# One layer of a convolution / RWKV-7 / mixture-of-experts step: the first modulation rows in two halves, and the column sums of the convolution's norm in four strips

## The chip, the cores and the metric

One core of one Trainium2 chip runs the whole program. Everything is float32. The metric is the device time of one execution in microseconds (us); the kernel before takes 1237.24 us (median of 3 runs, 1237.11 to 1237.88).

## The reference, cut to what matters

Two streams of 128 tokens (prompt and latent, here `g` = 0 and 1) go through one layer. The layer's first product needs the modulated input `h`:

```python
mod = (silu(c) @ ada_w + ada_b).reshape(6, D)      # D = 1024; one row of conditioning per stream
sh1, sc1, gt1, sh2, sc2, gt2 = mod
h = rms_norm(x, pre_mix_g) * (1.0 + sc1) + sh1
proj = h @ w_in                                    # 2560 columns: conv value and gate, r, k, v
...
a = sigmoid(a0[d] + (h @ a1[d]) @ a2[d])           # low-rank maps w1, a1, g1: 384 columns in all
g = sigmoid(h @ g1) @ g2
...
mu = mean(u, axis=-1); var = mean((u - mu)**2, axis=-1)   # layer norm of the convolution, 512 channels
...
x = x + gt2 * rms_norm(routed_ffn(h2), post_ffn_g)  # 32 experts, each token takes 4
```

`routed_ffn` reads 12 MB of weights per expert (8 MB gate and up, 4 MB down), 384 MB in all.

## The kernel before, in words

There are five instruction streams with semaphores between them and no planner: the order on each engine is the order of the code. SyncE (`SP`) starts nearly all transfers, in program order. TensorE (`PE`) runs all products; a float32 product appears in the trace as two matmul records, a transpose as one.

**First stage (0 to 49 us).** `SP` loads `x0`, then the first 2048 columns of `ada_w` in 8 chunks of 1 MB (`ada0`, line 363; columns 0 to 1023 give the shift, 1024 to 2047 the scale), then `lora1` (1.5 MB, line 365), the small tables, and the five blocks of `w_in` (line 377). PE transposes the normalised input (line 674) and the bias and gain rows (line 680), then takes each `ada_w` chunk with four products that write 32 partitions each (line 687: `siluT` has 32 columns, and product `j` writes rows `32j` to `32j+31` of bank 0, so the four sit in four column strips of the array and run at the same time). The result is copied (DVE line 1488), turned by four small products (line 699) and combined on DVE (lines 1491, 1494) into `modT`, which holds per channel the scale and the shift. Then ACT (line 1117) and DVE (line 1500) make the 8 chunks of `hT` = scale times input plus shift, and PE multiplies them with `lora1` (line 707: two of three 128-column blocks; line 726: the third). ACT puts the three results into `mids` with tanh, copy and sigmoid (line 1140), and PE goes on with the second low-rank factors (line 733), whose 16 results ACT takes one by one (lines 1142, 1144). Then comes `h @ w_in` (line 746). `keep_clock` (line 694) is a product whose result nobody reads.

**Middle (49 to 319 us).** Projections, then four rounds `q` of the RWKV recurrence. A round inverts a triangular matrix in levels `lv` = 1 to 6 (lines 849, 858, 859 on PE; ACT line 1192 and DVE line 1659 take the results). Round `q = 3` also holds the convolution's layer norm: `conv_sum` (line 784) sums 4 blocks of 286 columns over all 128 partitions with four products on a matrix of ones, once for the mean (ahead of level 3) and once for the variance (in level 6). ACT takes the square root (line 1199), DVE the reciprocal (line 1702), scales (lines 1705, 1708), and ACT applies the sigmoid (line 1208).

**Experts (319 us to the end).** 32 experts in pairs; PE line 626 is gate and up, line 664 down. `SP` starts a transfer into a buffer once PE has used it (lines 345, 348, 351).

Of the kernel before, what the change touches and what calls it, by code (L numbers as in the profile page):

```python
# [24 lines left out]
P = 128  # L25
G = 2
# [74 lines left out]
def build(nc, x_in, cond_in, ada_w, mod_in, w_in, w_out, chan_in, lora1_in, w2_in, a2_in, g2_in,  # L101
          s0_in, router_w, router_b, w_gu, b_gu, w_down, b_down, const_in, level_in, part_in,
          y_prompt, y_sample, st_f, st_b):
    with ExitStack() as ctx:
# [54 lines left out]
        first_T = view(r_ra[:, 1024:1088], "p (n m j r) -> p n m j r", n=2, m=4, j=4)  # L159
        madd, mmul = (view(r_hT[:, 1024 * n:1024 * (n + 1)], "p (b n) -> p b n", b=2) for n in range(2))  # L160
# [60 lines left out]
        cvT = view(r_E[:, 0:1024], "p (q t) -> p q t", q=Q)  # L221

# [366 lines left out]
        def pe_pair(pe, base, i, last_pair=False, turn=0, late=(), first=False):  # L589
# [4 lines left out]
            for q in range(2):  # L594
                arrived, arrived_dn = n * 128 + (64 * q + 80), n * 16 + (64 - 16 * q + (0 if first else 16))
# [15 lines left out]
                for k in order:  # L611
# [3 lines left out]
                    if in_spare:  # L615
                        pe.wait_ge(in_gu[3 + k], 80)
                    if first and q == 1 and k == order[-1]:
                        pe.wait_ge(in_gu[7], 80)
                    if q in late and k in (2, 6):
                        pe.wait_ge(in_gu[2 if k == 2 else 3], turn * 96 + (32 * (2 * last_pair + q) + 16))  # L620
                    if last_pair and k == 7 and q == 1:
                        pe.wait_ge(in_gu[4], turn * 32 + 48)
# [46 lines left out]
        def _(pe):  # L669
            pe.wait_ge(s["in_const"], 16)  # L670
# [6 lines left out]
            pe.wait_ge(s["in_mod"], 64)  # L677
# [4 lines left out]
            last.then_inc(s["first_tr"], 1)  # L682
            pe.wait_ge(s["silu"], 1)
# [7 lines left out]
            def keep_clock(count):  # L691

                for _ in range(count):
                    pe.matmul(ps[7], ident, xn[:, 0, 0:512], start=True, stop=True)

            keep_clock(1)
            pe.wait_ge(s["mod0"], 1)
            for m in range(4):
# [1237 lines left out]
```

## Time and profile before

| | |
|---|---|
| median of 3 runs | 1237.24 us |
| the profiled execution, its time | 1238.3 us |
| its span (first to last instruction) | 1236.5 us |
| PE busy | 94% of the span |
| DMA share, mean rate | 9 tenths in most of the slices, 369 GB/s |
| chain that ended last | PE 52%, DMA 43%, DVE 3%, the rest 2% |
| largest wait in that chain | DMA into `ring` from `w_gu`, 38% |

The profiled execution is 1.8 us longer than its span. The chain that ended last is followed back from the last instruction to what released it at each step; the 40 slices of the page are 30.9 us each.

### The profile page before, as it was taken

What the parts mean: (1) busy time and instruction counts of PE and PEld (TensorE: products, weight loads), DVE (VectorE), ACT (ScalarE), POOL (GpSimd) and SP (SyncE); (2) the same over time, 40 slices, a digit from 0 to 9 for tenths busy, and PEclk for the clock granted to TensorE, in tenths of its full rate; (3) what the DMA queues carried; (4) which work ended last, traced back from release to release, by engine and by line L of the source; (5) the groups of instructions that cost most, each with busy time, mean ns of one, the idle gap of its engine ahead of it and who ended that gap; (6) DMA issues with size and microseconds to landing.
All of it is one profiled execution on the core that took longest, in us unless ns stands there. A gap on an engine that the chain in (4) does not pass through costs nothing.

```text
span 1236.5 us, 15201 instructions
## 1 busy us (share of the span) xinstructions
PE 1157.3 (94%) x6032; PEld 549.0 (44%) x6032; DVE 412.6 (33%) x939; ACT 201.9 (16%) x447; POOL 89.1 (7%) x120
## 2 busy tenths in 40 slices
PE   5999999999999999999999898999999998989997
PEld 2886898784443433233333333333433333333332
DVE  0598878765412121212212121212131221212123
ACT  2311334242211101010101111010101011111102
POOL 1002654330000000000000000000000000000000
PEclk9999999999999999999999999999999999999999
DMA  9900724667999999999999999999999999999996
GB/s 370 387 21 29 312 108 171 274 215 267 349 420 425 429 430 429 432 435 430 427 436 426 434 431 425 438 408 423 429 434 429 430 434 428 431 430 426 425 426 262
DMA packets 40086, 456.43 MB, mean 369 GB/s; under 512 B 5056, under 2 KB 5584, under 8 KB 16496
## 3 DMA queue, kind: packets, MB, share of 16 engines
q1 hardware_dynamic: 39256, 455.01, 87.8%
q0 software_dynamic: 480, 0.80, 0.2%
q8 instruction: 25, 0.41, 0.1%
q10 hardware_dynamic: 312, 0.11, 0.0%
q14 instruction: 13, 0.11, 0.0%
HBM read 454.56 MB, written 1.34 MB: 369 GB/s over the span
## 4 chain that ended last, share of the span: by engine, by line
PE 52%; DMA 43%; DVE 3%; issue 1%; ACT 1%; SPq 0%; DVEq 0%; ACTq 0%
DMA ring<-in_w_gu 38%; PE bank L626 24%; PE bank L664 5%; PE bank L746 4%; DMA front<-in_w_down 3%; DMA ring<-in_ada_w 2%; PE bank L849 2%; PE bank L859 2%; PE bank L960 2%; PE bank L581 1%; PE bank L858 1%; PE bank L571 1%; PE bank L756 1%; PE bank L741 1%; PE bank L798 1%
## 5 line engine op out<-in xcount | busy, mean ns | idle before, releaser
L626 PE MATMUL bank<-ring,front 128*64 128x512 f32 x2032 | 461.3, 609 | 35.4 <-DMA ring<-in_w_gu 35.4
L626 PEld LDWEIGHTS bank<-ring,front 128*64 128x64 f32 x2032 | 144.0, 140 | 350.4 <-issue 284.1
L1443 DVE TENSOR_SCALAR front<-bank 128x512 f32<-128x512 f32 x32 | 22.1, 691 | 481.0 <-PE bank L626 481.0
L664 PE MATMUL bank<-front 128*64 128x512 f32 x512 | 113.6, 595 | 9.5 <-ACT front L1091 9.1
L664 PE MATMUL bank<-ring,front 128*64 128x512 f32 x512 | 113.4, 595 | 5.1 <-ACT front L1091 5.1
L1083 ACT ACTIVATE front<-front 128x512 f32<-128x512 f32 x32 | 20.2, 631 | 487.4 <-DVE front L1443 487.4
L1467 DVE COPY front<-bank 64x512 f32<-64x512 f32 x32 | 21.9, 683 | 175.1 <-PE bank L664 175.1
L664 PEld LDWEIGHTS bank<-front 128*64 128x64 f32 x512 | 36.3, 137 | 76.5 <-issue 73.3
L664 PEld LDWEIGHTS bank<-ring,front 128*64 128x64 f32 x512 | 36.3, 137 | 71.9 <-issue 70.4
L581 PE MATMUL bank<-front 128*128 128x512 f32 x136 | 62.9, 605 | 1.1 <-DVE front L1467 1.1
L1561 DVE SCALAR_TENSOR_TENSOR front<-front 128x286 f32<-128x286 f32 x120 | 58.8, 538 | 0.5
L571 PE MATMUL bank<-front 128*128 128x128 f32 x480 | 56.1, 275 | 0.0
L746 PE MATMUL bank<-front,ring 128*128 128x256 f32 x256 | 55.5, 379 | 0.0
L1094 ACT ACTIVATE front<-bank 64x512 f32<-64x512 f32 x32 | 19.0, 593 | 223.6 <-PE bank L664 223.6
L571 PEld LDWEIGHTS bank<-front 128*128 128x128 f32 x480 | 54.8, 192 | 0.0
L746 PEld LDWEIGHTS bank<-front,ring 128*128 128x128 f32 x256 | 48.6, 190 | 6.9 <-ACT front L1144 0.3
L1659 DVE TENSOR_TENSOR ring<-bank,front 128x256 f32<-128x256 f32 x96 | 39.3, 420 | 21.8 <-PE bank L859 14.2
L581 PEld LDWEIGHTS bank<-front 128*128 128x128 f32 x136 | 24.4, 189 | 39.3 <-issue 39.3
L1378 POOL TENSOR_TENSOR ring<-ring,front 128x256 f32<-128x256 f32 x48 | 36.3, 770 | 66.8 <-DVE ring L1651 57.1
L1420 DVE TENSOR_TENSOR front<-front,bank 128x512 f32<-128x512 f32 x64 | 39.4, 677 | 0.0
L849 PE MATMUL bank<-ring 128*128 128x128 f32 x192 | 37.6, 281 | 0.3
L859 PE MATMUL bank<-ring 128*128 128x128 f32 x192 | 36.6, 277 | 0.0
(259 smaller groups left out, 1000.0 us busy)
## 6 DMA issues: line engine op xcount, KB each, us to landing
ring<-in_w_gu SPq DMA_DIRECT2D x46, 4096.0 KB
front<-in_w_down SPq DMA_DIRECT2D x30, 2048.0 KB, 19.5
ring<-in_w_down SPq DMA_DIRECT2D x28, 2048.0 KB, 20.2
ring<-in_w_gu SPq DMA_DIRECT2D x25, 2048.0 KB
ring<-in_ada_w SPq DMA_DIRECT2D x24, 1024.0 KB, 10.3
ring<-in_w_gu SPq DMA_DIRECT2D x20, 1024.0 KB
ring<-in_w_in SPq DMA_DIRECT2D x5, 2048.0 KB, 19.8
ring<-in_w_down SPq DMA_DIRECT2D x6, 1024.0 KB, 9.6
```

The lines of the kernel that those rows point to most:

```text
L571: last = pe.matmul(ps[4 + c // 4][:, (c % 4) * P:(c % 4 + 1) * P], h2[:, g, c * P:(c + 1) * P], sel[:, g].rearrange("p q s -> p (q s)"), s ...
L581: pe.matmul(ps[4 + 2 * g + c], GT[:, g, :], outp[:, c * 512:(c + 1) * 512], start=not on_sums, stop=True, skip_group_check=on_sums).then_i ...
L626: last = pe.matmul(ps[r][64 * hf:64 * hf + 64, :], xT[:, k, S * q:S * q + S], rows, start=False, stop=(k == order[-1]))
L664: last = pe.matmul(ps[2][64 * c:64 * c + 64, :], actT[:, m, 64 * hf:64 * hf + 64], wdn[q][hf][:, m, c * 512:(c + 1) * 512], start=(k == 0) ...
L746: last = pe.matmul(out[:, 0:N], win[kind][:, k, q * P:(q + 1) * P], hT[:, k, :], start=(k == 0), stop=(k == KC - 1))
L849: pe.matmul(ps[c % 2][:, 0:T], LTn[:, lv % 2, g, h, :], YX[:, c, 1, :], start=True, stop=True) .then_inc(s["p_mm"], 1)
L859: pe.matmul(ps[2 + c][:, 0:T], Pn[:, c, :], YX[:, c, 0, :], start=False, stop=(lv == LEVELS - 1), skip_group_check=True).then_inc(s["e_mm" ...
L960: last = pe.matmul(ps[2 * g + c], lhs, wout[:, k, c * 512:(c + 1) * 512], start=(k == 0), stop=(k == KC - 1))
L1378: po.tensor_tensor(LTn[:, lv % 2, g], LT[:, g, :, 0, 3, :], level_mask[lv - 1].unsqueeze(1).broadcast_to([P, 2, T]), ALU.mult).then_inc(s[ ...
L1420: v.tensor_tensor(yacc[:, g, c * 512:(c + 1) * 512], yacc[:, g, c * 512:(c + 1) * 512], ps[4 + 2 * g + c], ALU.add).then_inc(s["y_added"], 1)
L1561: v.scalar_tensor_tensor(acc[:, c, :], u[:, c, tap:tap + A_COLS], wcol, acc[:, c, :], ALU.mult, ALU.add).then_inc(s["conv"], 1)
L1659: v.tensor_tensor(YX[:, c], ps[2 + c][:, 0:2 * T].rearrange("p (a t) -> p a t", a=2), side_mask[lv].unsqueeze(1).broadcast_to([P, 2, T]), ...
```

## The change

Three things, and what hangs on them:

1. **`ada_w` in halves.** `SP` loads the scale half of each of the 8 chunks (0.5 MB each), then `lora1`, then the 8 shift halves, each behind a wait for the scale half of its chunk. ACT's transfer of the bias and gain rows becomes 8 pieces instead of 4. PE makes the scale rows, `hT` is first made without the shift, and `lora1` is multiplied with that. The products of the shift half stand between those of `lora1`. The missing part, shift times `lora1`, is a row of 384 numbers per stream (`brow`): PE makes it in four strips from `shP` and `lora1`, ACT copies it, and three products add it to the three accumulators. DVE adds the shift to `hT` itself afterwards, for `w_in`. `k`, `r` and `v` of `w_in` now wait for both halves.
2. **Column sums in strips.** `conv_sum` becomes `conv_part` (four products of 32 output partitions each) and, after a copy by ACT, `conv_sum(n)` (one product that adds the strips). DVE subtracts the mean one level later.
3. Counts of shared semaphores are raised where the expert part waits on the same ones.

The core of the diff (the raised counts and the renamed views are left out):

```diff
@@ SyncE
-                sp.dma_start(ada0[:, k, :], ada_w[k * P:(k + 1) * P, 0:2048]).then_inc(in_ada0[k], 16)
+                sp.dma_start(ada0[:, k, D:2 * D], ada_w[k * P:(k + 1) * P, D:2 * D]).then_inc(in_ada0[k], 16)
             for hf in range(2):
                 sp.dma_start(lora1[:, 4 * hf:4 * hf + 4, :], lora1_in[:, 4 * hf:4 * hf + 4, :])\
                     .then_inc(s["in_lora_b" if hf else "in_lora"], 16)
+            for k in range(KC):
+                sp.wait_ge(in_ada0[k], 16)
+                sp.dma_start(ada0[:, k, 0:D], ada_w[k * P:(k + 1) * P, 0:D]).then_inc(in_ada0[k], 16)
...
-                    sp.wait_ge(s["ada0_acc"], KC)
+                    sp.wait_ge(s["ada0_acc"], 2 * KC)
@@ TensorE
+            def condition(k, at):
+                for j in range(4):
+                    last = pe.matmul(ps[0][32 * j:32 * j + 32, at:at + 256], siluT[:, k, :],
+                                     ada0[:, k, 4 * at + 256 * j:4 * at + 256 * j + 256],
+                                     start=(k == 0), stop=(k == KC - 1), skip_group_check=True)
+                last.then_inc(s["ada0_acc"], 1)
...
             for k in range(KC):
                 pe.wait_ge(in_ada0[k], 16)
-                for j in range(4):
-                    last = pe.matmul(ps[0][32 * j:32 * j + 32, :], siluT[:, k, :], ada0[:, k, j * 512:(j + 1) * 512],
-                                     start=(k == 0), stop=(k == KC - 1), skip_group_check=True)
-                last.then_inc(s["ada0_acc"], 1)
+                condition(k, 256)
+            keep_clock(ps[7])
             pe.wait_ge(s["mod0"], 1)
+            turn_rows((2, 3))
+            keep_clock(ps[7])
...
                 for n in range(2):
+                    pe.matmul(bank_of(n)[:, 0:N], lora1[:, k, n * P:(n + 1) * P], hT[:, k, :], start=(k == 0), stop=False)
+                shifts(*{3: (0,), 5: (1,), 7: (2, 3)}.get(k, ()))
+            for k in range(KC):
+                pe.matmul(bank_of(2)[:, 0:N], lora1[:, k, 2 * P:3 * P], hT[:, k, :], start=(k == 0), stop=False)
+                shifts(*{1: (4,), 4: (5,), 7: (6, 7)}.get(k, ()))
+            keep_clock(ps[1])
+            pe.wait_ge(s["mod0"], 2)
+            turn_rows((0, 1))
+            keep_clock(ps[1], 256)
+            pe.wait_ge(s["modT"], 2)
+            for k in range(KC):
+                t = k % 4
+                last = pe.matmul(ps[0][32 * t:32 * t + 32, 0:3 * P], shP[:, k, :], lora1[:, k, :],
+                                 start=(k < 4), stop=(k >= 4), skip_group_check=True)
+            last.then_inc(s["mod0_tr"], 1)
+            keep_clock(ps[1], 256)
+            pe.wait_ge(s["in_rw"], 32)
+            pe.wait_ge(s["mod0"], 3)
+            for n in range(3):
+                pe.matmul(bank_of(n)[:, 0:N], brow[:, n * P:(n + 1) * P],
+                          const[:, K_E2:K_E2 + G].unsqueeze(2).broadcast_to([P, G, T]), start=False, stop=True)\
+                    .then_inc(s["l2_mm"], 1)
...
-                    last = pe.matmul(ps[7][:, 0:A_COLS], ones, src[:, q, :], start=(q == 0), stop=(q == Q - 1))
+                    last = pe.matmul(ps[7][32 * q:32 * q + 32, 0:A_COLS], ones[:, 0:32], src[:, q, :], start=True, stop=True)
+            def conv_sum(n):
+                pe.wait_ge(s["c_std"], n)
+                pe.matmul(ps[7][:, 0:A_COLS], one_of_32, cpart, start=True, stop=True).then_inc(s["cs_mm"], 1)
@@ ScalarE
-                             scale=modT[:, m, 2 * (2 + hf):2 * (2 + hf) + 1],
-                             bias=modT[:, m, 2 * hf:2 * hf + 1]).then_inc(s["hT_a"], 1)
+                             scale=modT[:, 2 + m, G * j:G * j + 1]).then_inc(s["hT_a"], 1)
+            a.wait_ge(s["mod0_tr"], 3)
+            a.activation(brow, ps[0][:, 0:3 * P], ACT.Copy).then_inc(s["mod0"], 1)
...
+                        if q == Q - 1 and (lv, c) in ((3, 0), (LEVELS - 1, 2)):
+                            a.wait_ge(s["cs_mm"], 1 if lv == 3 else 3)
+                            a.activation(cpart, ps[7][:, 0:A_COLS], ACT.Copy).then_inc(s["c_std"], 1)
@@ VectorE
+            v.wait_ge(s["ada0_acc"], 2 * KC)
+            v.tensor_copy(mod0[:, 0:256], ps[0][:, 0:256]).then_inc(s["mod0"], 1)
...
+            for c in range(0, KC, 2):
+                two = hT[:, c:c + 2, :].rearrange("p c (g t) -> p c g t", g=G)
+                v.tensor_tensor(two, two, shP[:, c:c + 2, 0:G].unsqueeze(3).broadcast_to([P, 2, G, T]), ALU.add)\
+                    .then_inc(s["hT_v"], 1)
```

How it moves PE's instructions. In the first stage before, PE's queue between the last conditioning chunk and the first products of `lora1` (L707; the last word of a row names what it waits for, `in_wide_k` is the semaphore of chunk `k`):

```order
L687 MATMUL bank<-ring,front 32x512 [waits in_wide_7]
L687 MATMUL bank<-ring,front 32x512 x3
L694 MATMUL bank<-front 128x512
L699 MATMUL bank<-front 128x8 [waits mod0]
L699 MATMUL bank<-front 128x8 x3
L694 MATMUL bank<-front 128x512
L707 MATMUL bank<-front 128x256 [waits hT_v,hT_a,in_lora]
```

In the change, the end of the same stage, from the last two shift chunks (L698) to the second low-rank factors (L767):

```order
L698 MATMUL bank<-ring,front 32x256 [waits in_wide_6]
L698 MATMUL bank<-ring,front 32x256 x3
L698 MATMUL bank<-ring,front 32x256 [waits in_wide_7]
L698 MATMUL bank<-ring,front 32x256 x3
L679 MATMUL bank<-front 128x512
L706 MATMUL bank<-front 128x8 [waits mod0]
L706 MATMUL bank<-front 128x8
L679 MATMUL bank<-front 128x256
L741 MATMUL bank<-front 32x384 [waits modT]
L741 MATMUL bank<-front 32x384 x7
L679 MATMUL bank<-front 128x256
L748 MATMUL bank<-front 128x256 [waits mod0,in_rw]
```

The copy, the turning and the way back from DVE stood once, ahead of the products of `lora1`; now they stand twice, and the second time a further product (L741), ACT's copy of it and a third step on PE (L748) follow before the low-rank stage can go on.

In round 3, level 6, PE's queue around the variance before (L849 is a level's first product, L859 its last; L784 the sum):

```order
L849 MATMUL bank0<-ring 128x128 [waits p_ev,ltn,yx_ev]
L784 MATMUL bank7<-front 128x286 [waits c_sq]
L784 MATMUL bank7<-front 128x286 x3
L859 MATMUL bank2<-ring 128x128 [waits p_ev]
L849 MATMUL bank1<-ring 128x128 [waits p_ev,ltn,yx_ev]
```

and in the change (L820 the strips, L826 the sum of the strips, L890 and L900 the level's products):

```order
L890 MATMUL bank0<-ring 128x128 [waits p_ev,ltn,yx_ev]
L820 MATMUL bank7<-front 32x286 [waits c_sq]
L820 MATMUL bank7<-front 32x286 x3
L900 MATMUL bank2<-ring 128x128 [waits p_ev]
L890 MATMUL bank1<-ring 128x128 [waits p_ev,ltn,yx_ev]
L900 MATMUL bank3<-ring 128x128 [waits p_ev]
L826 MATMUL bank7<-front 128x286 [waits c_std]
```

The four products stay where they were, with 32 output partitions instead of 128, and one product with a wait for ACT's copy (`c_std`) comes in three products later.

## Rows read from the trace of the kernel before

**Rows 1.** The page: slices of 30.9 us, and the chain that ended last.
```profile
PEclk9999999999999999999999999999999999999999
DMA  9900724667999999999999999999999999999996
...
PE 52%; DMA 43%; DVE 3%; issue 1%; ACT 1%; SPq 0%; DVEq 0%; ACTq 0%
```

**Rows 2.** Windows: us; busy (count) of PE, PEld, DVE, ACT, POOL; PEclk, DMA share, GB/s.
```profile
324.00:327.00 3.00, 3.00 (x18) 1.00 (x16) 0.00 (x0) 0.00 (x0) 0.00 (x0) 1.00 0.98 309
330.00:333.00 3.00, 3.00 (x16) 0.77 (x12) 0.69 (x1) 0.01 (x1) 0.00 (x0) 1.00 1.00 423
```

**Rows 3.** Timeline, 0 to 60 us: start us, us, engine, line, op, count [idle before].
```profile
1.68 1.48 ACTq L1102 DMA_DIRECT2D front<-in_mod  x4
...
5.96 1.06 ACT L1108 ACTIVATE front<-front 128x1024 f32<-128x1024 f32 x1 [1.25 <-DMA front<-in_x]
...
8.30 1.28 ACT L1111 ACT_TABLE_LOAD   x1
9.60 0.29 ACT L1111 ACTIVATE front<-front 128x2 f32<-128x2 f32 x1
...
16.86 4.50 PE L687 MATMUL bank<-ring,front 128*32 128x512 f32 x40
...
18.17 0.13 PEld L687 LDWEIGHTS bank<-ring,front 128*32 128x32 f32 x4 [0.30 <-issue]
18.60 0.13 PEld L687 LDWEIGHTS bank<-ring,front 128*32 128x32 f32 x4 [0.30 <-issue]
...
25.26 1.94 PE L687 MATMUL bank<-ring,front 128*32 128x512 f32 x8 [1.42 <-DMA ring<-in_ada_w]
...
27.75 1.94 PE L687 MATMUL bank<-ring,front 128*32 128x512 f32 x8 [0.56 <-DMA ring<-in_ada_w]
...
29.75 0.69 DVE L1488 COPY front<-bank 128x512 f32<-128x512 f32 x1 [12.44 <-PE bank L687]
...
32.58 0.19 DVE L1491 TENSOR_TENSOR front<-bank,front 128x32 f32<-128x32 f32 x1 [2.14 <-PE bank L699]
...
33.65 7.14 PE L707 MATMUL bank<-front 128*128 128x256 f32 x32
...
40.46 0.76 ACT L1140 ACTIVATE front<-bank 128x256 f32<-128x256 f32 x2 [4.47 <-PE bank L707]
40.63 3.62 PE L726 MATMUL bank<-front 128*128 128x256 f32 x16
41.23 1.28 ACT L1140 ACT_TABLE_LOAD   x1
44.28 0.38 ACT L1140 ACTIVATE front<-bank 128x256 f32<-128x256 f32 x1 [1.77 <-PE bank L726]
...
44.81 4.48 PE L733 MATMUL bank<-front 64*128 64x256 f32 x32 [0.57 <-ACT front L1140]
```

**Rows 4.** Windows, columns as in rows 2, of the first stage.
```profile
14.70:24.80 10.10, 7.72 (x67) 3.23 (x65) 0.35 (x3) 0.00 (x0) 0.00 (x0) 1.00 1.02 424
24.90:31.60 6.70, 5.79 (x20) 1.36 (x20) 0.69 (x1) 0.00 (x0) 0.00 (x0) 0.50 1.01 405
31.80:40.00 8.20, 8.05 (x39) 6.51 (x39) 3.02 (x10) 2.90 (x8) 0.48 (x2) 1.00 1.05 386
```

**Rows 5.** One line's durations: ns min/median/max, where strips and whole-array products change places.
```profile
L756 PE MATMUL bank<-ring,front x128: 592/592/617, 149.5 to 230.0; 128*32 128x512 f32 x128
L969 PE MATMUL bank<-front x8: 590/592/697, 304.5 to 308.9; 128*128 128x512 f32 x8
```

**Rows 6.** Timeline, narrow: the change from strips to the whole array, and back.
```profile
16.45 0.47 PE L680 MATMUL bank<-front 8*128 8x8 f32 x3
16.86 1.07 PE L687 MATMUL bank<-ring,front 128*32 128x512 f32 x8
...
306.35 0.64 PE L987 MATMUL bank<-front 128*32 128x128 f32 x16
...
306.93 0.70 PE L969 MATMUL bank<-front 128*128 128x512 f32 x1
```

**Rows 7.** Timeline, 250 to 271 us: the two column sums and what follows.
```profile
251.06 2.09 PE L784 MATMUL bank<-front 128*128 128x286 f32 x8
...
262.17 2.10 PE L784 MATMUL bank<-front 128*128 128x286 f32 x8
...
264.52 1.53 DVE L1662 TENSOR_TENSOR ring<-bank,front 128x256 f32<-128x256 f32 x4 [2.20 <-PE bank L859]
...
264.92 0.49 ACT L1199 ACTIVATE front<-bank,front 128x286 f32<-128x286 f32 x1
...
265.97 1.93 DVE L1702 RECIPROCAL front<-front 128x286 f32<-128x286 f32 x1
```

More of the change, by code:

```diff
@@ L669, in _, with keep_clock @@
         def _(pe):
+            def keep_clock(bank, cols=512):
+                pe.matmul(bank[:, 0:cols], ident, xn[:, 0, 0:cols], start=True, stop=True)
             pe.wait_ge(s["in_const"], 16)
@@ L682, in _, with turn_rows, shifts @@
             last.then_inc(s["first_tr"], 1)
+            def condition(k, at):
[4 more added lines that the diff above has]
+                last.then_inc(s["ada0_acc"], 1)
+            def turn_rows(ms):
+                for m in ms:
+                    last = pe.matmul(ps[0][:, m * 8:(m + 1) * 8], mod0[:, m * P:(m + 1) * P], used_rows, start=True, stop=True)
+                last.then_inc(s["mod0_tr"], 1)
+            def shifts(*chunks):
+                for k in chunks:
+                    pe.wait_ge(in_ada0[k], 32)
+                    condition(k, 0)
             pe.wait_ge(s["silu"], 1)
@@ L685, in _ @@
                 pe.wait_ge(in_ada0[k], 16)
-                for j in range(4):
-                    last = pe.matmul(ps[0][32 * j:32 * j + 32, :], siluT[:, k, :], ada0[:, k, j * 512:(j + 1) * 512],
-                                     start=(k == 0), stop=(k == KC - 1), skip_group_check=True)
-                last.then_inc(s["ada0_acc"], 1)
[L691 to L696, printed above, removed]
+                condition(k, 256)
+            keep_clock(ps[7])
             pe.wait_ge(s["mod0"], 1)
-            for m in range(4):
-                last = pe.matmul(ps[0][:, m * 8:(m + 1) * 8], mod0[:, m * P:(m + 1) * P], used_rows, start=True, stop=True)
-            last.then_inc(s["mod0_tr"], 1)
-            keep_clock(1)
+            turn_rows((2, 3))
+            keep_clock(ps[7])
+            pe.wait_ge(s["modT"], 1)
             for k in range(KC):
@@ L723, in _ @@
                         pe.wait_ge(s["kk"], emptied(n - 7, "v"))
-                if kind == "l1":
-                    for k in range(KC):
-                        last = pe.matmul(out[:, 0:N], lora1[:, k, q * P:(q + 1) * P], hT[:, k, :],
-                                         start=(k == 0), stop=(k == KC - 1))
-                elif kind in "wa":
+                if kind in "wa":
                     pe.wait_ge(s["in_lora2"], 48)
@@ L907, in _ @@
                         level_update(q, lv, 1)
+                        if lv == 3 and q == Q - 1:
+                            conv_sum(1)
                         level_product(q, lv, 3)
@@ L1101, in _ @@
             for j in range(4):
-                a.dma_start(first[G * j:G * j + G], mod_in[:, 32 * j:32 * j + G, 0:512].rearrange("n r c -> r n c"))\
-                    .then_inc(s["in_mod"], 16)
+                for half in range(2):
+                    r, c = 32 * (2 * half + j // 2), 256 * (j % 2)
+                    a.dma_start(first[G * j:G * j + G, :, 256 * half:256 * half + 256],
+                                mod_in[:, r:r + G, c:c + 256].rearrange("n r c -> r n c")).then_inc(s["in_mod"], 16)
             a.wait_ge(s["in_cond"], 16)
@@ L1294, in _ @@
             po.memset(siluT, 0.0).then_inc(s["silu_pad"], 1)
+            po.memset(shP, 0.0).then_inc(s["silu_pad"], 1)
             po.memset(r_u, 0.0)
@@ L1692, in _ @@
                         norm_bonus(q - 1)
-                    if q == Q - 1 and lv in (2, 3):
-                        v.wait_ge(s["cs_mm"], 1)
-                        for c in (2 * lv - 4, 2 * lv - 3):
+                    if q == Q - 1 and lv in (3, 4):
+                        v.wait_ge(s["cs_mm"], 2)
+                        for c in (2 * lv - 6, 2 * lv - 5):
                             v.scalar_tensor_tensor(acc[:, c, :], ps[7][:, 0:A_COLS], -1.0 / CH, acc[:, c, :],
```

74 lines of the change are left out of this document (41 added, 33 removed).

## The prediction, before the run

> **What bounds the kernel now.** I read the page first: DMA is at nine tenths from slice 10 to the end, and the chain that ended last is PE and DMA alone [rows 1]. So the question is where the DMA stream of the experts starts. The windows from 324 us show it at 0.98 and then 1.00 of its share while PE still runs without a pause [rows 2]: from 330 us on the queue is never empty, each of its early transfers is released by PE, and PE before 319 us is what releases the first. A microsecond that PE's chain gains or loses before 319 us moves the end by a microsecond; nothing the change does after that point moves anything. Second I read the timeline of the first stage, where the change works. PE waits there for `ada_w`: chunks come every 2.49 us (25.26 and 27.75), the last at 27.75, and between its end at 29.69 and the first product of `lora1` at 33.65 lie a copy, the turning and DVE's steps [rows 3]. PE ran much of that at the lower clock: the granted clock was 1.00 to 24.8 us, 0.50 from 24.9 to 31.6 us, and 1.00 again after (2.4, 1.2 and 2.4 GHz) [rows 4]. From 33.65 to 44.25 us PE is busy with `lora1`, and the second low-rank factors start at 44.81 us [rows 3]. That start is the mark for the first stage: what follows it is the same in both kernels. Third I read the timeline of round 3, where both column sums stand in PE's queue with nothing beside them, 2.1 us each, and the second is followed by the square root and the reciprocal at 265.97 us [rows 7].
>
> **The change, first stage.** All times are those of the profiled execution.
>
> *Start of the scale half.* Eight chunks of 0.5 MB instead of 1 MB free 4 x 2.49 = 10.0 us of transfer: the last lands at 27.75 - 10.0 = 17.8 us. PE is then the later one. It reaches the first chunk at 16.86 us; a round of four strips over 512 columns takes 0.43 us (18.17 to 18.60) [rows 3], over 256 columns 0.215 us. Eight chunks of two rounds are 3.44 us, to 20.3 us. The tail of a product is 0.16 us (592 ns long, 430 ns apart) [rows 3, 5]. Copy, turning and DVE: `keep_clock` holds PE until 20.3 + 0.2 + 0.86 = 21.4 us, four turning records of 0.11 us and the tail lead to 22.0 us, and from DVE's start to the first product of `lora1` it is 33.65 - 32.58 = 1.07 us as before [rows 3]. `lora1` starts at 23.1 us, 10.5 us earlier than before, and both its halves (3.7 us behind the scale half at 424 GB/s [rows 4]) are there by 21.6 us. The four more pieces of bias and gain rows lie on ACT: four took 1.48 us, and ACT then waited 1.25 us for `x0` [rows 3], so I cost them at nothing; without that cover they would be 1.5 us.
>
> *What gives it back.* (a) The same products of `lora1` take 7.14 and 3.62 us less one overlap, 10.4 us to the last start-to-start step [rows 3]. (b) The shift half's 16 rounds are now on the path and no longer under a transfer: 3.44 us. (c) Its chunks stand in six groups, and each group is a change from whole-array products to strips and back. What a change costs is seen in three places. Into strips: three records 0.11 us apart begin at 16.45 us, so 16.79 us was due and 16.86 us came [rows 6], and the first round takes 617 instead of 592 ns [rows 5]; elsewhere it is some 20 ns more, so 0.12 us. Out of strips: L987's four rounds of 0.11 us end their steps at 306.83 us, the next product starts at 306.93 us [rows 6] and is 697 instead of 592 ns long [rows 5], so 0.20 us. Six times in and five times out until the last shift round are 1.7 us. The stream ends at 23.1 + 10.4 + 3.4 + 1.7 = 38.7 us. The last shift chunk lands at 21.6 + 10.0 = 31.6 us, well before it is due, at about 38 us. (d) The second way round: `keep_clock` and its entry to 39.8 us, turning and DVE to 40.75 us, strips of 384 columns (four rounds of 0.32 us, with entry and tail 1.6 us) to 42.3 us, ACT's copy of 384 columns with its wait 0.55 us (a little over the 0.49 us of 286 columns [rows 7]), the way back to PE 0.15 us as from 44.66 to 44.81 us [rows 3]: the three adding products start at 43.0 us. (e) The first of them is through at 43.6 us and ACT takes two blocks in 0.76 us, to 44.4 us. Then comes a cost that was hidden: the table load of 1.28 us ran at 41.23 us under the third block's 3.62 us of products [rows 3]. What follows a load starts at once (8.30 + 1.28, and 9.60 us [rows 3]). Now the three results come 0.43 us apart and nothing covers it. 44.4 + 1.28 + 0.38 + 0.15 = 46.3 us against 44.81 us: the first stage **loses 1.5 us**.
>
> The adding of the shift to `hT` is four DVE instructions of 512 columns, 0.7 us each as the copy of 512 [rows 3], from 41 us; the first product that needs it comes near 50 us, so it costs nothing, and if that cover were gone 2.8 us. `SP` waits for a scale chunk before each shift chunk, with `lora1` queued behind that chunk; the bytes ahead of `w_in` are the same, so its blocks land as before, and `k`'s longer wait (from 29.7 to 38.9 us) ends while the two blocks ahead of it still run.
>
> Of the change between strips and whole products the trace gives 0.3 us a pair, by which six groups, the `shP` strips and both column sums cost 2.9 us. The Trainium skill, TensorEngine Tiling (Array Packing), section "Key Properties", says that changing the tiling mode, and not just the tile, drains TensorE; it gives no figure. Taken as one tail of 0.16 us for every change, an estimate from the rows, the six groups and the two sums would cost 18 x 0.16 = 2.9 us: rule and row agree here, and a sum made as if strips were free would put the first stage at a gain of 0.5 us instead.
>
> **The change, column sums.** Eight records of 286 columns take 1.93 us (2.10 less the tail) [rows 7], 0.24 us each. Now two rounds of strips are 0.48 us, in and out 0.32 us, and the adding product 0.48 us: 1.28 us, a gain of 0.65 us for the first. The second is followed by DVE: before, PE's first update waited out the whole sum, and the reciprocal began 3.8 us after the sum's start (262.17 to 265.97) [rows 7]. Now that update starts after 0.8 us, DVE takes four results of 0.38 us (1.53 us for four [rows 7]), the third held up by the adding product, and the reciprocal begins after 3.1 us, with the square root (0.49 us [rows 7]) just ahead of it: 0.7 us. ACT's two copies of 0.43 us lie in its pauses. Together a **gain of 1.35 us**. The bounds: nothing, if copies and waits eat it; 2.0 us, if strips cost nothing to enter and leave.
>
> **Sum.** +1.5 - 1.35 = +0.15 us. The profiled execution would take 1238.3 + 0.15 = 1238.45 us; it stood 1.1 us above the median, so the median becomes **1237.4 us**. The smallest difference I count as one is 0.2%, 2.5 us.
>
> **The rivals.**
> - *Strips are nearly free.* If the reloading of the weights is hidden in the change's longer rounds, the first stage gains 0.5 us and the sums 2.0 us: 1234.7 us, faster. For it: four weight loads lie inside each round. Against: every change of form in rows 5 and 6 shows a price. Chance 0.12.
> - *The clock falls (the other side, slower).* PE would have nothing between about 44.5 and 46.3 us while ACT loads its table, and short pauses in the second way round before it; then come the `w_in` products, which are bound by PE. Before, the clock fell after pauses of 1.4 us in every 2.5 us and stayed at 0.50 for 6.8 us [rows 3, 4]. The same stretch, if PE were busy in all of it, would cost half of itself, 3.4 us: 1240.8 us. It makes the kernel slower by over 0.2% from 4.7 us at the lower level on. Against: that fall followed several pauses in a row, this is one. Chance 0.10.
> - *The second way round is longer than I count* (each step between engines 0.2 us more, ten steps, or ACT's copies in level 3 and 6 hold PE): +2 us, 1239.4 us, still within 0.2%. Chance 0.18.
> - *The change doesn't do what it says:* a chunk of half the bytes needs the same 2.49 us. The last shift chunk would land at 31.5 + 8 x 2.49 = 51.4 us and the mark at 59 us: +14 us, 1251 us. Against: `w_in`, which comes in rows of 2 KB, runs at 386 GB/s [rows 4], the halves have 4 KB. Chance 0.02.
>
> **How the numbers follow.** The forecast has 0.58 and 1236.3 to 1238.6 us for itself. From 1235.2 to 1240.2 us lie the forecast, the third rival and part of the first two; 0.2 is left out. Faster by over 0.2% (below 1234.8): most of the first rival, 0.10. Slower by over 0.2% (above 1239.7): the second and fourth rival and a tail of the third, 0.16. Within: 0.74.
>
> **What would show it.** Right: the first product of `lora1` near 23 us, the last shift round near 38.7 us, ACT's table load in the open, the second factors' start (mark) near 46.3 us, the reciprocal 3.1 us after the variance strips, the granted clock 1.00 from 14.7 us to the experts, DMA full from 330 us. Wrong: a mark before 45 us, a reciprocal that is under 2.7 us or over 3.8 us behind the strips, a clock of 0.50 between 40 and 55 us, or a pause of PE before a shift chunk that DMA ends.

## The result, and the profile after

| | before | changed |
|---|---|---|
| median (lowest to highest), runs | 1237.22 us (1235.37 to 1242.09), 20 | 1239.46 us (1237.05 to 1246.03), 20 |
| the profiled execution, its time | 1238.3 us | 1243.65 us |
| its span | 1236.5 us | 1241.9 us |

The ratio is 1.0022 with an interval of 1.0012 to 1.0032: 2.2 us longer between the medians, where +0.15 us was forecast. The median lies inside the outer range of the forecast (1235.2 to 1240.2 us) and outside the 1236.3 to 1238.6 us that the forecast had for itself. It equals the 1239.4 us of the third rival by luck, since the second way round, which that rival makes longer, takes what the forecast gave it (see below). The profiled execution is far from the median of its kernel this time, and the runs of the change lie in two groups: eleven of the twenty from 1237.05 to 1239.51 us, nine from 1241.36 to 1246.03 us, none between. The profile is of the upper group, and so it shows what a median hides.

The page of the changed kernel, the lines that answer to [rows 1]:

```profile
PEclk9999999999999999999999999999999999999999
DMA  9900734567999999999999999999999999999995
...
PE 57%; DMA 38%; DVE 3%; ACT 1%; issue 1%; SPq 0%; DVEq 0%; ACTq 0%
```

The bound is the same: DMA is full from slice 10 on. At that scale nothing else can be seen; the clock line reads 9 throughout. The timeline of the changed kernel, TensorE and ACT in the first stage (start us, us, engine, line, operation, count, idle before it and what ended it), answers to [rows 3]:

```profile
11.93 3.65 PE L685 MATMUL bank<-front 128*128 128x128 f32 x16 [11.93 <-DVE front L1533]
15.50 3.58 PE L691 MATMUL bank<-front 8*128 8x8 f32 x16
19.01 5.73 PE L698 MATMUL bank<-ring,front 128*32 128x256 f32 x64
...
24.67 1.13 PE L679 MATMUL bank<-front 128*128 128x512 f32 x2
...
27.28 3.69 PE L729 MATMUL bank<-front 128*128 128x256 f32 x16 [0.18 <-ACT front L1164]
...
47.20 1.54 PE L748 MATMUL bank<-front 128*128 128x256 f32 x6
...
48.75 1.28 ACT L1189 ACT_TABLE_LOAD   x1
...
50.57 4.49 PE L767 MATMUL bank<-front 64*128 64x256 f32 x32 [1.82 <-ACT front L1189]
```

The mark, the start of the second low-rank factors, is at 50.57 us (L767) instead of 44.81 us: +5.76 us, where +1.5 us was forecast. Read it in pieces. From the first product of `lora1` (L729) to the mark it is 50.57 - 27.28 = 23.29 us; the forecast had 46.3 - 23.1 = 23.2 us. That part holds. The first product itself is 4.2 us late, at 27.28 instead of 23.1 us, and the reason stands in the first three rows. The 16 transposes (L685), the 16 products that turn the bias and gain rows (L691) and the 64 strip records of the scale half (L698) run one after the other with no pause and no wait, and simply take long: 3.65, 3.58 and 5.73 us. The forecast had taken 16.86 us for the start of the strips and 3.44 us for their rounds.

Whether that is the clock can be read in the steps of L698. Two windows of the same timeline, 22.6 to 23.1 us and 23.4 to 23.7 us; a row lists every record that runs in its window, so the two rows share some:

```profile
22.00 1.45 PE L698 MATMUL bank<-ring,front 128*32 128x256 f32 x12
```
```profile
22.85 1.03 PE L698 MATMUL bank<-ring,front 128*32 128x256 f32 x12
```

Both are three rounds of four records. Less the tail of 0.16 us the first three take 1.29 us, 0.43 us each, the other three 0.87 us: one of 0.43 and two of 0.22 us. So TensorE went from 1.2 to 2.4 GHz at 23.3 us. The view of windows gives 1.00 for all of this stretch; up to the first change in an execution that column does not show the level, and the durations do (here 0.43 us for a round at 1.00, and 0.22 us for the same round at 1.00).

The end of the first half, in narrow windows of the timeline of TensorE around the first expert product, before and then changed:

```profile
319.12 0.65 PE L626 MATMUL bank<-ring,front 128*64 128x512 f32 x2
```
```profile
323.53 0.65 PE L633 MATMUL bank<-ring,front 128*64 128x512 f32 x2
```

From the mark to the first expert product it is 274.31 us before and 272.96 us now: -1.35 us, the forecast gain of the column sums to the hundredth. And DMA starts as before, later by the same amount. The changed kernel, windows laid 4.4 us after those of [rows 2]:

```profile
328.40:331.40 3.00, 3.00 (x18) 1.00 (x16) 0.00 (x0) 0.00 (x0) 0.00 (x0) 1.00 1.00 314
334.40:337.40 3.00, 3.00 (x16) 0.77 (x12) 0.69 (x1) 0.01 (x1) 0.00 (x0) 1.00 1.03 434
```

The spans differ by 5.4 us: +5.76 in the first stage, -1.35 in the middle, +1.0 in the expert part (917.4 us before, 918.4 us now). That last part is the same code; over all profiles of this study it takes between 915.6 and 918.5 us with no relation to the kernel, so a single span says little about differences under some 3 us. The starts of single products say more.

The theory to test: **the terms of the sum are right, and what was missed is when the clock rises.** The rivals: the strips cost something else than 0.3 us a pair; ACT's table load is not what delays the mark; the strips in the column sums cost something in the experts' part.

### The profile page after: what moved, and what is told of

Read it like the earlier page. It is cut to its first block, busy times and chain, and to the rows that moved or that the text cites. A ratio compares the mean times of both kernels' runs of the same rounds, so it can differ in the third digit from the quotient of the medians.

```text
span 1241.9 us, 15419 instructions
## 1 busy us (share of the span) xinstructions
PE 1163.7 (94%) x6128; PEld 552.6 (44%) x6128; DVE 415.0 (33%) x945; ACT 202.5 (16%) x450; POOL 89.6 (7%) x121
## 4 chain that ended last, share of the span: by engine, by line
PE 57%; DMA 38%; DVE 3%; ACT 1%; issue 1%; SPq 0%; DVEq 0%; ACTq 0%
DMA ring<-in_w_gu 35%; PE bank L633 25%; PE bank L671 6%; PE bank L782 4%; DMA front<-in_w_down 3%; PE bank L588 2%; PE bank L900 2%; PE bank L890 2%; PE bank L1005 2%; PE bank L899 1%; PE bank L578 1%; PE bank L792 1%; PE bank L775 1%; PE bank L839 1%; PE bank L613 1%
## 5 line engine op out<-in xcount | busy, mean ns | idle before, releaser
L890 PE MATMUL bank<-ring 128*128 128x128 f32 x192 | 37.7, 282 | 0.3
L900 PE MATMUL bank<-ring 128*128 128x128 f32 x192 | 36.6, 277 | 0.0
```

What stands on the lines that cost most here:

```text
L890: pe.matmul(ps[c % 2][:, 0:T], LTn[:, lv % 2, g, h, :], YX[:, c, 1, :], start=True, stop=True) .then_inc(s["p_mm"], 1)
L900: pe.matmul(ps[2 + c][:, 0:T], Pn[:, c, :], YX[:, c, 0, :], start=False, stop=(lv == LEVELS - 1), skip_group_check=True).then_inc(s["e_mm" ...
```

## The experiments

Times of first products are read from each kernel's timeline. "Expert" is the first expert product, "full" the moment from which TensorE's steps are those of 2.4 GHz; in the last column the medians, each with its ratio to the kernel before on the same chip. The kernel before was run again beside each set: its median was 1237.24 us beside the second run of the changed kernel and e1 to e3, 1237.12 us beside e4 to e7, 1236.67 us beside e8 and e9. The ratio is estimated from all runs and differs a little from the quotient of two medians.

| kernel | full from | first `lora1` product | mark | expert | median us, ratio |
|---|---|---|---|---|---|
| before | 14.6; 1.2 GHz 24.9 to 31.7 | 33.65 | 44.81 | 319.12 | 1237.22 |
| changed | 23.3 | 27.28 | 50.57 | 323.53 | 1239.46, 1.0022 [1.0012, 1.0032] |
| changed, again | 24.5; 1.2 GHz 51.8 to 55.2 | 27.78 | 51.07 | 325.06 | 1239.55, 1.0020 [1.0005, 1.0034] |
| e1 | 9.6 | 21.59 | 44.88 | 317.85 | 1237.79, 1.0001 [0.9990, 1.0012] |
| e2 | 23.8 | 31.80 | 42.96 | 315.94 | 1236.75, 1.0000 [0.9984, 1.0016] |
| e3 | 14.7 | 23.09 | 46.38 | 320.75 | 1242.99, 1.0037 [1.0021, 1.0053] |
| e4 | 10.2; 1.2 GHz 27.3 to 37.6 | 35.74 | 47.73 | 322.03 | 1239.13, 1.0005 [0.9991, 1.0020] |
| e5 | 11.2 | 21.60 | 43.22 | 316.16 | 1235.15, 0.9982 [0.9970, 0.9995] |
| e6 | 11.7 | 21.68 | 43.67 | 316.61 | 1235.46, 0.9988 [0.9977, 0.9999] |
| e7 | 11.4 | 21.57 | 41.88 | 314.83 | 1234.49, 0.9972 [0.9960, 0.9983] |
| e8 | 12.8 | 32.83 | 44.00 | 318.34 | 1238.07, 1.0012 [1.0001, 1.0022] |
| e9 | 9.8 | 32.61 | 43.78 | 316.75 | 1237.19, 1.0002 [0.9992, 1.0012] |

**The changed kernel again**, with no edit.

> The changed kernel once more, to see the granted clock of the first stage in a second profile. Theory A (cold start: everything PE does from its first transposes on is now on the path, at whichever clock it is granted, where before a wait for ada_w hid it): the start of the second low-rank factors (the mark) lies between 45.1 us (clock full from the first product) and 50.6 us (full only from 23 us on), and it moves with the moment of the rise; the median is 1237.5 to 1241 us. Rival B (the loss is in the expert part, not ahead of it): the mark is near 50.6 us in every profile whatever the clock, and the time from the first expert to the end differs from before by over 1 us.

The late rise is no accident of one execution: strips at 18.76 us, full from 24.5 us, first `lora1` product at 27.78 us. The mark, at 51.07 us, is 0.5 us outside the expected stretch, because the clock rose 1.2 us later still. Both profiles rose late, so this run alone doesn't separate the theory from rival B; the time from the first expert product to the end (917.8 us, before 917.4 us) speaks against the rival, and e1 and e3 decide. Again two groups: seven of twelve runs up to 1239.8 us, five from 1241.42 us, and again the profiled one (1244.81 us) is of the upper. This execution also shows what the forecast's second rival had in mind. Two views of this kernel: the timeline at the mark, and the windows view of a stretch that begins 0.8 us after it:

```profile
51.07 1.55 PE L767 MATMUL bank<-front 64*128 64x256 f32 x8 [1.82 <-ACT front L1189]
```
```profile
51.90:55.10 3.20, 3.20 (x18) 3.20 (x17) 2.57 (x16) 3.17 (x9) 0.00 (x0) 0.50 1.05 388
```

The granted clock is 0.50 for 3.4 us. From the mark to the first expert product it takes 273.99 us instead of 272.96: the fall cost 1.0 us. None of the other profiles of the changed order has it at this place (changed, e1, e3, e5, e6, e7), although the pause ahead of the mark is the same 1.82 or 1.83 us in four of them.

**e1: TensorE busy before the first rows.** Eleven products that nobody reads, ahead of the transposes, while TensorE has nothing to do.

```diff
             pe.wait_ge(s["in_const"], 16)
+            for _ in range(11):
+                pe.matmul(ps[7][:, 0:P], ident, ident, start=True, stop=True)
             pe.wait_ge(s["xn"], 2)
```

> The changed kernel with 11 products of ident with itself ahead of the transposes, as soon as ident is loaded; their result is read by nobody. Theory A: the clock is full before or during the transposes, 16 transposes take about 1.9 us instead of 3.65, the turned rows 2.0 instead of 3.6 us, the mark comes at 45 to 46.5 us, and the median falls by 2 to 4 us against the changed kernel, to about 1236.3 us, with a smaller spread. Rival B: mark and median stay.

The timeline of this kernel, the rows that answer to those of the changed kernel:

```profile
6.47 4.18 PE L683 MATMUL bank<-front 128*128 128x128 f32 x22 [6.47 <-DMA front<-in_const]
11.61 1.97 PE L687 MATMUL bank<-front 128*128 128x128 f32 x16 [0.96 <-DVE front L1535]
13.51 1.95 PE L693 MATMUL bank<-front 8*128 8x8 f32 x16
15.38 3.66 PE L700 MATMUL bank<-ring,front 128*32 128x256 f32 x64
...
21.59 3.69 PE L731 MATMUL bank<-front 128*128 128x256 f32 x16 [0.18 <-ACT front L1166]
...
44.88 1.44 PE L769 MATMUL bank<-front 64*128 64x256 f32 x10 [1.83 <-ACT front L1191]
```

The three stretches take 1.97, 1.95 and 3.66 us instead of 3.65, 3.58 and 5.73 us: the same instructions at the other level of the clock. From there the distance is that of the changed kernel (21.59 to 44.88 us: 23.29 us in both). The mark falls from 50.57 to 44.88 us, and the runs lie within 1.9 us (1237.02 to 1238.90) instead of 9.0 us: the upper group is gone, and it stays away in e5, e6 and e7, which have the same eleven products (36 more runs, each kernel within 3.9 us). This is what the theory said. The mark is 0.1 us below the expected 45 to 46.5 us. The median, 1237.79 us, is 1.8 us below that of the changed kernel beside it, where 2 to 4 us were expected. Against the kernel before it is no gain (ratio 1.0001), although the first expert product comes 1.27 us earlier than in before's profile. That may lie in the expert part, which varies by up to 2.9 us between profiles, or in executions of before that were not profiled; that is not settled.

**e2: the column sums alone,** on the kernel before.

```diff
-                    last = pe.matmul(ps[7][:, 0:A_COLS], ones, src[:, q, :], start=(q == 0), stop=(q == Q - 1))
+                    last = pe.matmul(ps[7][32 * q:32 * q + 32, 0:A_COLS], ones[:, 0:32], src[:, q, :], start=True, stop=True)
...
+                pe.wait_ge(s["c_std"], n)
+                pe.matmul(ps[7][:, 0:A_COLS], one_of_32, cpart, start=True, stop=True).then_inc(s["cs_mm"], 1)
```

> The kernel before with the column sums in strips alone. Theory A and the prediction's second term: 1.35 us less up to the first expert (317.8 instead of 319.2 us in the trace), ratio 0.9989, the reciprocal 3.1 us behind the start of the variance strips. Rival C (the sums' gain is eaten by ACT's copies or lost before the experts): no difference at the first expert, ratio 1.000.

Mark to expert is 315.94 - 42.96 = 272.98 us, again 1.33 us less than before: the gain stands on its own in the trace. The runs can't show it: the ratio is 1.0000 with an interval of 0.9984 to 1.0016, which holds the expected 0.9989 and the rival's 1.000 alike. The surprise is in the first stage, which is that of the kernel before, to the instruction. The timeline of e2:

```profile
11.69 3.65 PE L676 MATMUL bank<-front 128*128 128x128 f32 x16 [11.69 <-DVE front L1494]
15.26 3.58 PE L682 MATMUL bank<-front 8*128 8x8 f32 x16
18.77 8.71 PE L689 MATMUL bank<-ring,front 128*32 128x512 f32 x56
27.75 1.06 PE L689 MATMUL bank<-ring,front 128*32 128x512 f32 x8 [0.27 <-DMA ring<-in_ada_w]
...
31.80 7.14 PE L709 MATMUL bank<-front 128*128 128x256 f32 x32
...
42.96 0.88 PE L735 MATMUL bank<-front 64*128 64x256 f32 x5 [0.56 <-ACT front L1151]
```

Here the clock rose late too, and it did no harm: TensorE is behind the chunks for 8.7 us, works them off (x56 without a pause) and has caught up at 27.75 us, when the last chunk lands as in [rows 3]. And it never paused ahead of that chunk, and the clock did not fall at 24.9 us (that the two belong together is tested in e8): the last eight strips take 1.06 instead of 1.94 us, and the mark is at 42.96 instead of 44.81 us. So between these profiles a late rise is worth a gain of 1.85 us in the old order, and a loss of 4.2 us in the new one. The profiled execution is near the fastest of its kernel (1233.93 us, lowest 1233.56). The twelve runs reach up to 1241.64 us, and those of before, 34 beside these, from 1235.26 to 1241.12 us. Two profiles 1.85 us apart don't account for such a spread; where it comes from in the old order is open.

**e3: the first stage alone.** The changed kernel with the column sums put back.

```diff
-                    last = pe.matmul(ps[7][32 * q:32 * q + 32, 0:A_COLS], ones[:, 0:32], src[:, q, :], start=True, stop=True)
+                    last = pe.matmul(ps[7][:, 0:A_COLS], ones, src[:, q, :], start=(q == 0), stop=(q == Q - 1))
```

> The changed kernel with the column sums as before (the first stage's change alone). Prediction's terms with theory A: 1.35 us more than the changed kernel at the same clock, so 1239 us when the clock rises early and up to 1243.5 us when it rises late. Rival C: the same as the changed kernel.

By chance this profile caught an early rise (14.7 us, as in the profile of before), without any added product. Its timeline:

```profile
11.68 3.40 PE L685 MATMUL bank<-front 128*128 128x128 f32 x16 [11.68 <-DVE front L1521]
15.01 1.95 PE L691 MATMUL bank<-front 8*128 8x8 f32 x16
16.89 3.66 PE L698 MATMUL bank<-ring,front 128*32 128x256 f32 x64
20.48 1.12 PE L679 MATMUL bank<-front 128*128 128x512 f32 x2
...
23.09 3.69 PE L729 MATMUL bank<-front 128*128 128x256 f32 x16 [0.18 <-ACT front L1155]
...
46.38 1.31 PE L767 MATMUL bank<-front 64*128 64x256 f32 x9 [1.83 <-ACT front L1180]
```

23.09 and 46.38 us, against 23.1 and 46.3 us of the forecast: with the clock that the forecast assumed, its sum comes out. The runs are again in two groups, four of eleven from 1238.16 to 1239.29 us, the profiled one (1238.68 us) among them, and seven from 1242.63 to 1245.44 us, up to 1.9 us above the expected 1243.5 us. Without the added products, both profiles of the new order with a late rise are thus of an upper group, and the one with an early rise is of a lower one. For the runs that were not profiled this is an inference. It is borne out by the distance between the medians of the two groups, 4.3 us (changed), 5.1 us (again) and 4.8 us (e3), where the rise moves the first `lora1` product by 4.2 and 4.7 us. The shares differ between kernels (4 of 11 here, 11 of 20 and 7 of 12 for the changed one), which is how this median comes to stand 3.5 us above that of the changed kernel although the column sums are worth 1.35 us in the trace. Group by group the two kernels differ by 0.2 and 0.7 us, less than these 1.35 us.

**e4: the eleven products ahead of the kernel before.** If an early rise is what helps, does it help the old order?

> The kernel before with the same 11 products ahead of the transposes. Theory A: before, PE's start is hidden by the wait for ada_w, so an early rise gives nothing, and the pauses of the wait then always bring the lower clock between the last chunks: the mark stays at 44.8 us or up to 0.5 us around it in the profile, and the median is 1237.2 to 1238.5 us, with fewer fast executions than before. Rival B: a full clock from the start helps any kernel, median 1.5 us or more under before.

It doesn't, and the expectation missed. The timeline of e4:

```profile
20.45 1.06 PE L689 MATMUL bank<-ring,front 128*32 128x512 f32 x8 [1.20 <-DMA ring<-in_ada_w]
...
26.25 1.07 PE L689 MATMUL bank<-ring,front 128*32 128x512 f32 x8 [2.25 <-DMA ring<-in_ada_w]
28.59 1.94 PE L689 MATMUL bank<-ring,front 128*32 128x512 f32 x8 [1.27 <-DMA ring<-in_ada_w]
...
35.74 7.97 PE L709 MATMUL bank<-front 128*128 128x256 f32 x32
...
47.73 0.58 PE L735 MATMUL bank<-front 64*128 64x256 f32 x2 [0.56 <-ACT front L1142]
```

and its windows:

```profile
10.30:27.20 16.90, 11.34 (x96) 5.64 (x94) 1.81 (x6) 1.34 (x2) 0.00 (x0) 1.00 1.01 415
27.40:37.50 10.10, 8.91 (x25) 4.77 (x26) 3.71 (x11) 2.90 (x8) 0.48 (x2) 0.50 1.03 392
```

TensorE is fast early, so it waits for each of the last four chunks, up to 2.25 us at a time, and then the clock falls for 10.3 us, across the turning and the first products of `lora1`. The mark is 2.9 us later than before. Not all of that is the clock: the last chunk is taken at 28.59 instead of 27.75 us, 0.84 us later, and the remaining 2.1 us lie between it and the mark, where the lower level lasts longer. In the runs the loss is not clear of noise (ratio 1.0005, interval 0.9991 to 1.0020; the median, 1239.13 us, is 0.6 us above the expected stretch), but rival B's gain is refuted. The Trainium skill, TensorE: Matmul & The Clock Gate, section "Loop structure matters more than you think", warns of a loop in which a long DMA wait stands between the products, since they then run at the low clock; these rows agree, with pauses of 1.20 to 2.25 us ahead of the stretch at 0.50.

**e5: all shift chunks in one group,** on e1.

```diff
-                shifts(*{3: (0,), 5: (1,), 7: (2, 3)}.get(k, ()))
...
-                shifts(*{1: (4,), 4: (5,), 7: (6, 7)}.get(k, ()))
+            shifts(*range(KC))
```

> e1_warm with all eight shift chunks in one group behind the third block of lora1 instead of six groups. Prediction's term (0.32 us for each change into strips and back): five pairs less, mark at 43.3 us instead of 44.88, first expert at 316.25 instead of 317.85 us. Rival D (the change of form costs little, the stretch is long for another reason): mark within 0.4 us of 44.88.

The timeline of e5:

```profile
21.60 7.14 PE L731 MATMUL bank<-front 128*128 128x256 f32 x32 [0.18 <-ACT front L1165]
...
32.13 3.66 PE L700 MATMUL bank<-ring,front 128*32 128x256 f32 x64
35.72 1.13 PE L679 MATMUL bank<-front 128*128 128x512 f32 x2
...
43.22 1.10 PE L768 MATMUL bank<-front 64*128 64x256 f32 x7 [1.82 <-ACT front L1190]
```

The same products take 35.72 - 21.60 = 14.12 us, where e1 takes 37.38 - 21.59 = 15.79 us (its `keep_clock` starts at 37.38 us). Five groups fewer, 1.67 us: 0.33 us for a change into strips and back, against 0.32 us read from [rows 5, 6]. It also refutes the first rival. The Trainium skill, TensorEngine Tiling (Array Packing), section "Key Properties", says that a change of the tiling mode drains TensorE; these rows agree in that a change has its price, 0.33 us for both ways together.

**e6: no table load between the results,** on e1. The tanh is made from the sigmoid, and DVE corrects it: tanh(x) = 2 sigmoid(2x) - 1. Not shown in the cut: PE waits for DVE's step, and an early activation whose result nobody reads, which stands ahead of the stage to bring in the table, is a sigmoid instead of a tanh.

```diff
-                    ins = a.activation(mids[:, q, :], out[:, 0:N], (ACT.Tanh, ACT.Copy, ACT.Sigmoid)[q])
+                    ins = a.activation(mids[:, q, :], out[:, 0:N], (ACT.Sigmoid, ACT.Copy, ACT.Sigmoid)[q], scale=(2.0, 1.0, 1.0)[q])
...
+            v.tensor_scalar(mids[:, 0, :], mids[:, 0, :], 2.0, -1.0, ALU.mult, ALU.add).then_inc(s["first_tr"], 1)
```

> e1_warm with tanh(x) computed as 2 sigmoid(2x) - 1 (the second step on DVE), so that ACT needs no table load behind the second block. Prediction's term: the load of 1.28 us is in the open, mark at 43.6 us instead of 44.88. Rival E (something else ends last there, DVE's added step or the third product): mark at 44.5 us or later.

The timeline of e6 around the mark:

```profile
41.61 1.54 PE L750 MATMUL bank<-front 128*128 128x256 f32 x6
42.38 1.19 ACT L1192 ACTIVATE front<-bank 128x256 f32<-128x256 f32 x3 [0.91 <-PE bank L750]
42.79 0.29 DVE L1572 TENSOR_SCALAR front<-front 128x256 f32<-128x256 f32 x1 [1.10 <-ACT front L1192]
...
43.67 1.10 PE L770 MATMUL bank<-front 64*128 64x256 f32 x7 [0.52 <-ACT front L1192]
```

ACT takes the three results in a row, TensorE's pause goes from 1.83 to 0.52 us. With 0.09 us of later start taken off (21.68 against 21.59 us at L731) the mark comes 1.30 us earlier, and the load takes 1.28 us.

**e7: e5 and e6 together.**

> e1_warm with both: one group and no table load. Theory A with both terms: mark at 42.0 us, first expert at 315.0 us, median 1234.9 us. If the two overlap, the mark lies between 42.0 and 43.3 us.

The mark is at 41.88 us, 3.0 us before that of e1: both add up, and this is 2.9 us before that of the kernel before. With the column sums the first expert product starts at 314.83 us instead of 319.12. The median is 1234.49 us (1232.62 to 1236.37) against 1237.12 us of the kernel before in the same runs, a ratio of 0.9972 [0.9960, 0.9983]: 0.3% faster than the kernel before, beside which the changed kernel stood at 1.0022.

**e8: the old order with its pauses filled,** e4 with a product that nobody reads behind each of the chunks 2 to 6. **e9** is the same with the column sums of e2.

```diff
                 last.then_inc(s["ada0_acc"], 1)
+                if 2 <= k < KC - 1:
+                    pe.matmul(ps[7], ident, xn[:, 0, 0:512], start=True, stop=True)
```

> e4_before_warm with one product that nobody reads (ident with the input, 512 columns, 0.86 us at full clock) behind each of the chunks 2 to 6 of ada_w, while PE waits for the next one. Theory A: the clock stays full until the last chunk, the first product of lora1 comes at 31.8 us (as in the profile of e2_conv_only, where the rise came late and no fall followed), the mark at 43.0 us instead of 44.81 (before) or 47.73 (e4), and the median falls to 1235.5 to 1236.3 us. Rival F: the fall is not what costs the time there, and the mark stays near 44.8 us.

> e8_before_fill with the column sums in strips: the change's second part on the kernel before, with the clock held. Theory A and the term of 1.35 us: mark 43.0 us, first expert at 315.9 to 316.1 us, median 1234.2 to 1235.2 us, so within 1 us of e7_all (first expert 314.83 us, median 1234.49 us) without the halves. Rival C: no gain against e8_before_fill.

The pauses shrink to 0.4 us and less, and the clock doesn't fall. The timeline of e8:

```profile
28.79 1.06 PE L689 MATMUL bank<-ring,front 128*32 128x512 f32 x8 [0.37 <-DMA ring<-in_ada_w]
...
32.83 7.14 PE L711 MATMUL bank<-front 128*128 128x256 f32 x32
...
44.00 4.27 PE L737 MATMUL bank<-front 64*128 64x256 f32 x31 [0.57 <-ACT front L1144]
```

But the last chunk is taken at 28.79 us (28.57 in e9), 1.0 and 0.8 us later than in before and e2, and the marks miss the expected one by that. The medians miss too: 1238.07 us for e8, where 1235.5 to 1236.3 us were expected and the kernel before took 1236.67 us beside it, so e8 is 0.1% slower; and 1237.19 us for e9, where 1234.2 to 1235.2 us were expected. The strips of the column sums are there again: from the mark to the first expert product 274.34 us in e8, 272.97 us in e9. In all three kernels of the old order with the eleven products the last chunk is late (28.59, 28.79 and 28.57 us, against 27.75 us in before and e2). Whether the added work delays the transfer or the executions only differ in it was not tried. What stands is that the pauses and the lower clock of the old order belong together (e4 against e8), and that its earliest mark is e2's, at a late rise. Filling the pauses is not shown to be of use.

## Why the prediction was right or wrong

- **What bounds the kernel:** right. Over the twelve profiles the first expert product lies between 314.83 and 325.06 us and the span between 1232.1 and 1242.9 us, and the line through them rises by 1.06 us of span for each microsecond (standard error 0.09).
- **Start of the scale half:** the step that failed. "It reaches the first chunk at 16.86 us; ... Eight chunks of two rounds are 3.44 us" takes the start from an execution whose clock rose at 14.6 us, and gives the moment of the rise no term and none of the rivals. The start had no weight before, since the old order waits for `ada_w` until 27.75 us whatever TensorE does first. The change takes this cover away: from the first transpose on, TensorE itself is the path, and with it the moment when its clock rises. With a rise at 23.3 us the stretch from the first transpose to `keep_clock` (L679) takes 24.67 - 11.93 = 12.74 us, in e3 20.48 - 11.68 = 8.80 us; with 0.25 us of later begin, that is the 4.2 us (27.28 against 23.09 us). The outer range held the median all the same, which is luck: by the two groups about half of the executions (18 of 32) had the early rise that the sum took for granted. That the four more pieces of bias and gain rows cost nothing was right (the transposes begin at 11.67, 11.68 and 11.93 us, 11.69 us before).
- **The parts of what gives it back:** right. Strips at 0.32 us a pair (0.33 in e5), the table load in the open at 1.28 us (1.30 in e6), from `lora1` to the mark 23.29 us against 23.2. Two slips are in the working: 44.4 + 1.28 + 0.38 + 0.15 is 46.2 and not 46.3 us, so its own terms give a loss of 1.4 us and a sum of +0.05 us; and the 18 changes of 0.16 us are those of the six groups, the two sums and the `shP` strips, which that sentence leaves out.
- **Column sums:** -1.35 us forecast, -1.35 us in the change and -1.33 us alone. In the runs the gain is smaller or lost in the spread (e2: ratio 1.0000; e9 is 0.9 us below e8). The reciprocal begins 2.97 us after the variance strips, where 3.1 us was forecast. The two rows, from two windows of the changed kernel's timeline:

```profile
267.40 0.69 PE L820 MATMUL bank<-front 128*32 128x286 f32 x8
```
```profile
270.37 1.93 DVE L1765 RECIPROCAL front<-front 128x286 f32<-128x286 f32 x1
```

- **From one execution to the median:** wrong as a step. "It stood 1.1 us above the median, so the median becomes 1237.4 us" holds only if both kernels see the same clock in the same way. With an early rise the first stages are 46.38 - 44.81 = +1.6 us apart, with a late one 50.57 - 42.96 = +7.6 us (e2 has before's first stage); less 1.35 us this makes +0.2 us and +6.3 us. The measured +2.2 us lies between. That fits a mixture but doesn't test it, since it isn't known in what share of before's executions the clock rises early, and each of these differences rests on one profile a side.
- **The rivals:** strips nearly free, refuted by e5. A fall of the clock near the mark: seen once, for 3.4 us and 1.0 us of time (the rival's half of the stretch would be 1.7 us), and not the cause; the rival had the right engine and the wrong end of the stage. The second way round longer: no, from the first product of `lora1` to the adding products it takes 47.20 - 27.28 = 19.92 us, where 43.0 - 23.1 = 19.9 us was forecast. That halves don't load faster: no, TensorE waits for no chunk.

## What to carry to other kernels

Before you shorten a wait, look at what lies ahead of it on the waiting engine: its durations cost nothing under the wait and everything without it, and at a kernel's start TensorE's are those of either clock. Give TensorE work from the first moment in an order that it bounds (e1 took 5.7 us off the profiled stage and the upper group off the runs). In an order that waits for transfers don't expect a gain from it (e4's mark came 2.9 us later in its profile, and its runs show no gain). A table load or a change of tiling that lay under other work becomes a term of the sum when that work moves: fold the functions into one table and the strips into one group first.

## What the runs showed of the hardware

Within the first 60 us: the clock of TensorE rose at 14.6, 14.7, 23.3, 23.8 and 24.5 us in five profiles in which TensorE had done the same since 11.7 to 11.9 us (transposes and products of 8 columns); with the eleven products, from 6.3 to 6.8 us on, it rose between 9.6 and 12.8 us in all seven. Without them the 16 transposes take 3.36 to 3.65 us, with them 1.97 us in e1 and e4; the turned rows take 1.95 or 3.58 us. It fell again after pauses in three executions (again, before, e4) and stayed down for 3.4, 6.8 and 10.3 us; the same pause of 1.8 us ahead of the mark had no fall behind it in four others. In the expert part every profile has eight to ten stretches of 3.4 us at 0.50, the first from 485.9 to 521.6 us on, depending on the profile. What decides between the early and the late rise is open.
